# Two of four query tiles turned in 32x32 blocks by VectorE and set in place through HBM, in an attention bound by TensorE

## What is computed

```python
qx = mla_queries(hx, mla_w_dq[j], mla_g_q[j], mla_w_uq[j], cos, sin)
kx, vx = mla_keys_values(hx, ..., cos, sin)
kc, vc = mla_keys_values(hc, ..., None, None)
ox = block_attention(qx, jnp.concatenate([kc, kx], axis=1), jnp.concatenate([vc, vx], axis=1))
x = x + g1 * (ox @ mla_w_o[j])

# block_attention, for each block of 128 queries
s = jnp.einsum('bqhd,bkhd->bhqk', qblk, k).astype(F32) * scale
p = jax.nn.softmax(s, axis=-1).astype(v.dtype)
return jnp.einsum('bhqk,bkhd->bqhd', p, v)

# modulation of each layer: 6 * 1024 numbers, each a product of a row of 1024 with silu(c)
mod_x = silu_c @ mod_w[i] + mod_b[i]
```

## Time and profile before

| what | value |
|---|---|
| median of three runs | 1644.83 us (1644.77 to 1646.06) |
| span of the profiled execution | 1645.5 us |
| TensorE busy | 1633.9 us (99%) |
| VectorE busy | 1043.6 us (63%) |
| GpSimd busy | 1026.5 us (62%) |
| ScalarE busy | 571.0 us (35%) |
| attention, first transpose of head 0 to the end of the last value product | 112.9 to 316.8 us |
| DMA | 220.61 MB, 134 GB/s on average |

### The profile page before, as it was taken

The page is one execution under the profiler, slowest core; times in us unless marked ns, Lnnn a source line. Parts: engine busy times, 40 slices in busy tenths (PEclk is TensorE's granted clock), DMA queues, the critical chain, the costliest instruction groups (busy, mean ns, idle before and its releaser), DMA issues.

```text
span 1645.5 us, 24018 instructions
## 1 busy us (share of the span) xinstructions
PE 1633.9 (99%) x8950; PEld 1364.2 (83%) x8950; DVE 1043.6 (63%) x1537; ACT 571.0 (35%) x1017; POOL 1026.5 (62%) x656
## 2 busy tenths in 40 slices
PE   9999999999999999999999999999999999999998
PEld 7887778798888888889887798888888898888887
DVE  3567777677877865635487566655558359746173
ACT  3467777633233232203344243222222121123111
POOL 3455766656666766575579456666676645567663
PEclk9999999999999999999999999999999999999999
DMA  9234335232269863435322233344434253223332
GB/s 371 87 90 129 111 106 165 79 93 96 89 211 320 298 225 103 141 137 172 120 90 65 77 99 102 125 156 140 153 106 143 97 214 120 65 84 103 91 101 90
DMA packets 59095, 220.61 MB, mean 134 GB/s; under 512 B 6849, under 2 KB 9153, under 8 KB 55682
## 3 DMA queue, kind: packets, MB, share of 16 engines
q1 hardware_dynamic: 53826, 204.96, 38.2%
q10 hardware_dynamic: 5184, 14.49, 2.3%
HBM read 201.07 MB, written 14.16 MB: 131 GB/s over the span
## 4 chain that ended last, share of the span: by engine, by line
PE 95%; DVE 4%; ACT 0%; issue 0%; DMA 0%; DVEq 0%; SPq 0%; ACTq 0%
PE PS L2444 28%; PE PS L2446 28%; PE PS L2445 28%; PE PS L2821 3%; PE PS L2783 2%; PE PS L1012 1%; PE PS L2430 1%; PE PS L1785 1%; PE PS L2595 1%; DVE SC L3572 0%; DVE WA L1990 0%; PE PS L1791 0%; DVE MR L3522 0%; PE PS L2720 0%; PE PS L2721 0%
## 5 line engine op out<-in xcount | busy, mean ns | idle before, releaser
L2354 POOL TENSOR_TENSOR WL<-RAW,WH 128x1024 fp32r<-128x1024 f32 (+3 forms) x211 | 542.8, 2572 | 17.6
L2444 PE MATMUL PS<-HH,WH 128*128 128x512 f32 (+1 forms) x1340 | 507.5, 379 | 0.0
L2446 PE MATMUL PS<-HH,WL 128*128 128x512 f32 (+1 forms) x1340 | 502.9, 375 | 0.0
L2445 PE MATMUL PS<-HL,WH 128*128 128x512 f32 (+1 forms) x1340 | 502.9, 375 | 0.0
L2351 POOL TENSOR_SCALAR WH<-RAW 128x1024 fp32r<-128x1024 f32 (+3 forms) x211 | 239.4, 1134 | 287.8 <-PE PS L2446 276.5
L2444 PEld LDWEIGHTS PS<-HH,WH 128*128 128x128 f32 x1340 | 252.2, 188 | 50.7 <-issue 6.2
L2446 PEld LDWEIGHTS PS<-HH,WL 128*128 128x128 f32 x1340 | 252.2, 188 | 45.9
L2445 PEld LDWEIGHTS PS<-HL,WH 128*128 128x128 f32 x1340 | 252.3, 188 | 43.9
L2379 POOL TENSOR_SCALAR PR<-PR,SC 128x768 f32<-128x768 f32 x47 | 107.3, 2292 | 66.7 <-DVE SC L3579 66.3
L2444 PE MATMUL PS<-HIDH,WH 128*128 128x512 f32 (+1 forms) x396 | 145.3, 367 | 0.0
L2445 PE MATMUL PS<-HIDL,WH 128*128 128x512 f32 (+1 forms) x396 | 144.8, 366 | 0.0
(11 more groups left out here) (532 smaller groups left out, 2894.6 us busy)
## 6 DMA issues: line engine op xcount, KB each, us to landing
RAW<-in_wup SPq DMA_DIRECT2D x88, 512.0 KB, 3.6
MRF<-in_modw SPq DMA_DIRECT2D x52, 512.0 KB, 4.8
RAW<-in_wdn SPq DMA_DIRECT2D x32, 704.0 KB, 4.1
...
MK<-in_modk SPq DMA_DIRECT2D x8, 1024.0 KB, 10.9
...
hy_hs<-HST ACTq DMA_DIRECT2D x4, 1024.0 KB, 4.0
```

Of the source, the lines that this page charges most:

```text
L2354: pool.tensor_tensor(WL[s][:, 0:n], raw[:, 0:n], WH[s][:, 0:n].bitcast(F32), ALU.subtract).then_inc(tile_split, 1)
L2444: pe.matmul(out, wh, xh, start=first, stop=False)
L2445: pe.matmul(out, wh, xl, start=False, stop=False)
L2446: return pe.matmul(out, wl, xh, start=False, stop=last)
```

## The change

Three things change in the attention; head 15 keeps the old way.

1. **Two query tiles (BLOCKED = 2) are turned by VectorE.** The exponential of qt 0 and 1 writes its columns in a permuted order: keys 4 apart come together (its source is read with a stride of four elements). GpSimd scales the tile as before. VectorE turns it in place in blocks of 32x32 (block_turn, one instruction of 128x768). SP stores both tiles to HBM (blocks_out, 384 KB each) and loads them back (blocks_in, 768 KB, 1024 runs of 768 bytes) so that each block lies on the partitions of its keys, in a new tile PB. TensorE turns only qt 2 and 3, twelve pieces a head instead of 24, and ScalarE copies them in three copies of 128x512 instead of six. The value product takes its first half of tokens from PB and its second from PT.
2. **The value product of head h moves to the beginning of stage h+1.** The twelve transposes stand as eight behind the second score and four at the end of the stage. The outputs' high parts and remainders move one stage on as well, and the output lies in bank 7. The chunks of projections are dealt anew between the scores; in odd heads and 14 the first stands ahead of the first score.
3. **24 modulation rows instead of 28 stand in the attention**: four ahead of head 0, two in head 0, two in each odd head, three in head 14 and one behind it. Four rows go to the first feed-forward stage, which begins its rows one step earlier (LATE 11 to 10).

Some semaphores are renamed or shared so that there is room for the new ones (turned, blocks_out, blocks_in); their waits stay equivalent. The second layer and the second block are as before.

```diff
-EARLY, LATE, LAST_ROWS = 28, 11, 88
+EARLY, LATE, LAST_ROWS = 24, 10, 88
+BLOCKED = 2
+PRE_ROWS = 4
+LAST_HEAD = HEADS - 1
...
-        PT = r.put("PT", [P, 6, L])
+        PB = r.put("PB", [P, BLOCKED, 4, 6, 32])
+        PT = r.put("PT", [P, 6, P * (4 - BLOCKED)])
+        PT_LAST = Region(pt_at).put("PT_LAST", [P, 6, L])
...
+            def blocks_out(h, qt):
+
+                sp.wait_ge(S["turned"], BLOCKED * h + qt + 1)
+                sp.dma_start(d_blocks[h % 2, qt, :, :], PR[h % 2][:, qt, :]).then_inc(S["blocks_out"], 16)
+
+            def blocks_in(h):
+
+                sp.wait_ge(S["pv"], h + 1)
+                sp.wait_ge(S["blocks_out"], 16 * BLOCKED * (h + 1))
+                sp.dma_start(PB[:, :, :, :, :].rearrange("p i m t j -> p (i m) (t j)"),
+                             d_blocks[h % 2].rearrange("i (m k) (c x) -> (k c) (i m) x", m=4, c=4)
+                             ).then_inc(S["blocks_in"], 16)
...
+            for h in range(LAST_HEAD):
+                for qt in range(BLOCKED):
+                    blocks_out(h, qt)
+                blocks_in(h)
+                if h == 0:
+                    two_rows(PRE_ROWS)
+                if h % 4 == 2 and h < 12:
+                    rope_move(h + 2, 2)
+                elif h % 4 == 3 and h < 12:
+                    rope_move(h + 3, 2)
+                if h % 2 == 0 and h < 10:
+                    head_weights(h // 2 + 3)
+                elif h == 10 or h == 12:
+                    ring("wo", a["wo"], h // 2 - 5)
+                if h % 2 == 0 and h < 14:
+                    two_rows(PRE_ROWS + 2 + h)
...
```

```diff
+                for kt in (2 * n, 2 * n + 1):
+                    for qt in range(BLOCKED, 4):
+                        q = (kt % 2) * 256 + (qt - BLOCKED) * P
+                        m = pe.transpose(PS[:, 6 + n % 2, q:q + P], PR[h % 2][:, qt, kt * P:(kt + 1) * P], IDENT[:, :])
+                m.then_inc(S["s_tr"], 1)
...
+                pe.wait_ge(S["pt"], 4 * h + 3)
                 v = slice(VH * h, VH * h + VH)
+                pe.wait_ge(S["blocks_in"], 16 * (h + 1))
                 for kt in range(6):
-                    pe.wait_ge(S["pt"], 7 * h + kt + 2)
+                    pe.wait_ge(S["pt"], 4 * h + kt // 2 + 2)
+                    pe.matmul(outputs(h, 0).rearrange("p (i m j) -> p i m j", i=2, m=4), V[:, kt, v],
+                              PB[:, :, :, kt, :], start=kt == 0, stop=kt == 5)
+                    m = pe.matmul(outputs(h, 1), V[:, kt, v], PT[:, kt, :], start=kt == 0, stop=kt == 5)
+                m.then_inc(S["pv"], 1)
...
             def head(h):
 
+                early = h % 2 or h == 14
                 if h:
-                    first_turns(h)
-                else:
-                    turn(h, 0)
-                    turn(h, 1)
+                    value(h - 1)
+                if early:
+                    chunk_between(h, 0)
                 for qt in range(4):
...
+                    score(h + 1, qt)
+                    if qt == 3 and h < 14 and h % 2 == 0:
+                        chunk_between(h, 3)
+                        project_keys(h // 2 + 1)
+                    elif qt < 3 or not early:
+                        chunk_between(h, qt + early)
+                    if qt == 1:
+                        turn(h, 0)
+                        turn(h, 1)
+                turn(h, 2)
```

```diff
-                act.activation(PR[h % 2][:, qt, :], wide(2 * (qt % 2), LK), ACT.Exp, bias=NMX[:, c:c + 1], scale=1.0,
+                out, src = PR[h % 2][:, qt, :], wide(2 * (qt % 2), LK)
+                if qt < BLOCKED and (per or h < LAST_HEAD):
+                    out, src = out.rearrange("p (c t j) -> p c t j", c=4, t=6), src.rearrange("p (t j c) -> p c t j", t=6, c=4)
+                act.activation(out, src, ACT.Exp, bias=NMX[:, c:c + 1], scale=1.0,
                                accum_out=SUMS[:, c:c + 1]).then_inc(S["sexp"], 1)
...
-                act.copy(PT[:, kt, :], bank(6 + kt % 2)).then_inc(S["pt"], 1)
...
+                act.copy(PT[:, 2 * n:2 * n + 2, :].rearrange("p k q -> p (k q)"), bank(6 + n % 2)).then_inc(S["pt"], 1)
...
+            def block_turn(h, qt, i=0, per=0):
+
+                dve.wait_ge(S["pnorm"], i * (3 * per) + (3 * h + qt if h else qt + 1))
+                dve.transpose(PR[h % 2][:, qt, :], PR[h % 2][:, qt, :]).then_inc(S["turned"], 1)
...
+                maximum(h + 1, 3, i, per)
+                if fourth:
+                    first_keys(h // 2 + 1, i, per)
+                inverse_sum(h + 1, 2, i, per)
+                if h < 14:
+                    block_turn(h + 1, 0, i, per)
...
+                if fourth:
+                    query_lo(h + 3, i, per)
+                elif first:
                     query_lo(h + 2, i, per)
+                if rows and h != 0:
+                    row(1)
+                inverse_sum(h + 1, 3, i, per)
+                if h < 14 and not fourth:
+                    block_turn(h + 1, 1, i, per)
                 if h < 14 and h % 2 == 0:
                     key_lo(h // 2 + 1, i, per)
-                if h % 2:
-                    row(1)
-                out_lo(h, i, per)
+                if fourth:
+                    block_turn(h + 1, 1, i, per)
+                if h == 14:
+                    row(2)
                 if h == 0:
                     query_lo(3)
-
-            dve.wait_ge(S["tab_in"], 64)
+                    row(1)
```

390 lines of the change are left out of this document (204 added, 186 removed).

## The result

| | before | after |
|---|---|---|
| median of the runs | 1645.44 us (1644.77 to 1647.85) | 1676.24 us (1672.97 to 1679.42) |
| ratio | | 1.0185, 95% interval 1.0169 to 1.0201 |
| span of the profiled execution | 1645.5 us | 1674.2 us |
| first to last value product | 189.0 us (125.04 to 314.02) | 213.1 us (123.57 to 336.69) |

A forecast was written before the change was run, and what follows sets the result against it. TensorE was taken to bound the kernel, with little room before VectorE. From 1645.5 us, 19.7 of transposes went off and 11.8 of waits came on: 1637.6 profiled, 1637 as the median, range 1628 to 1655.

The forecast's parts named there:

- The 180 transposes: Attention, TensorE: three groups of four transposes fewer a head, 1.3 us each in 15 heads, 19.7 us saved in all.
- The block turn: VectorE in the attention: one 128x768 instruction, two a head, assumed to take 0.955 us each.
- keys: Heads 4, 8, 12: key matmuls wait for the third tile's exponential, 1.1 us three times, 3.3 us.
- first score: Heads 5, 9, 13: the score needing both key remainders waits for VectorE, 0.8 us three times, 2.4 us.
- blocks in heads 5, 9 and 13: Value product waits for blocks reloaded from HBM after a late second turn, 0.7 us three times, 2.1 us.
- two passes: Rival: VectorE's turn passes its columns twice, taking 1.8 us, so VectorE becomes the bound; 1648 us, chance 0.13.
- The new trip through HBM: Attention: storing turned tiles takes 3 us, loading them 5, together 8; within an ordinary head's 10.5 to 13.5 us period, free.
- Slower, by the trip: Rival: store and reload take 12 us or more, every value product waits; 1655 us at 13 us, chance 0.14.
- as long as TensorE is as busy as this: Whole kernel: TensorE's granted clock is 1.00, the 2.4 GHz level, in every head and stays there under that condition.
- waits of 3 us in head 1: Head 1, once: SP's queue holds the first store behind a modulation load, so the value product waits 3.0 us.
- The wait behind the last copy: Value product waits for ScalarE's third wide copy, 0.15 us in seven heads, 1.0 us.
- the feed-forward stage, put at nothing: First FFN stage: four added modulation rows, 5.1 us of VectorE work, fit beside TensorE's 11 us and cost nothing.

## Why the prediction was wrong

**Right.** The 180 transposes went off TensorE. Their 19.7 us is the prediction's figure and no run measures it alone; from the prediction's own rows (0.36 us and 0.09 us a group) it comes to 20.2. The block turn (0.962 for 0.955), the load (4.8 for 5), the store alone (2.3 for 3) were priced well; the trip is 7 to 8 us where nothing stands beside it. Three of the named waits came with their size: keys 2.9 for 3.3, first score 2.5 for 2.4, blocks in heads 5, 9 and 13 2.5 for 2.1. The rival "two passes" is out.

**The step that failed most** is the sentence in "The new trip through HBM": in an ordinary head the trip has a whole period, "There the trip costs nothing", and the weights' loads "hide it". I compared the trip's own 8 us with the period and left out what is issued just ahead of it. I did look at SP's queue for the rope moves' issue time (2.3 us), and not at the 1.5 to 1.66 MB that follow them in heads 2, 6 and 10. A store behind them takes 7 to 9 us instead of 3. The trip is then 13.5 us (156.7 to 170.2), and the rival "Slower, by the trip", which named a load ahead in the queue, was right on the mechanism. It had the trip at 12 us or more, and measured are 13.5 to 15.2. It was wrong in its place and its price: not every head, but three of them, and head 14 behind the reloaded input.

**The second** is a term that was missing in the sum and in all rivals: what a pause does to the clock. The prediction said that the clock stays at its high level "as long as TensorE is as busy as this", and then added waits of 3 us in head 1 without asking that question. It cost 10.7 us, as much as the pauses of heads 3, 7 and 11. All pauses for the blocks and the low clock behind them are 32 us of the table. Without the trip 24 go, and some 8 stay as other waits, which these pauses had hidden.

**The third** is "covers": I counted what each transpose group cost and only twice asked what it had covered. The wait behind the last copy was put at 1.0 us; in the kernel without the trip, waits inside the products are 6 us. The kernel with neither trip nor turns gains nothing (1.0007): the reordering gives back, in waits, all that fewer transposes save.

**The fourth** is the feed-forward stage, put at nothing: 4.5 us, and 1.5 of low clock. I counted whether VectorE had the time for four rows there (it had), not whether the new phase of its small products against GpSimd's splits would hold up the residual. The Trainium skill (SBUF — State Buffer, "Who interferes with whom") states the rule that bears on it: VectorE's instruction with two inputs in SBUF and GpSimd's reads exclude each other for a whole instruction. The rows at 367 us agree (each product ends 0.02 to 0.03 us behind GpSimd's instruction). It was at work in the kernel before too, where it cost TensorE nothing.

**Chances and range.** Slower had 0.22; the range ended at 1655, which a kernel with an ideal trip would almost have filled (1652). The sum was made of separate waits, each at its own length; with the low clock behind them, the five long pauses cost 1.4 to 1.8 times theirs.
